# Two output projections in the other order, and the memory's rows in another buffer: a hybrid decoder block in float32 on one core

## The reference

```
hn = rms_norm(h)
z, xbc, dt, q, k, v, qi, ki, wi, g_ssd, g_attn = split(hn @ w_in)
y_ssd  = ssd_branch(z, xbc, dt)          # 256 x 2048, normed in 4 groups
y_attn = dsa_branch(q, k, v, qi, ki, wi) # 256 x 1024
merged = sigmoid(g_ssd) * (y_ssd @ w_ssd_o) + sigmoid(g_attn) * (y_attn @ w_attn_o)
h += merged @ w_out
mn = rms_norm(mem)                       # 256 memory tokens
h += cross_attention(rms_norm(h), mn, w_cq, w_ckv, w_co)
h += hier_moe(rms_norm(h))               # 4 groups of 8 experts, top 1 group, top 2 experts
```

## Time and profile before

| | us |
|---|---|
| median of 3 runs | 1519.66 |
| lowest, highest | 1517.8, 1520.55 |
| the profiled execution | 1519.16 |
| its span in the profile | 1517.3 |
| TensorE busy in the span | 1381.7 (91%) |
| VectorE, ScalarE busy | 845.1 (56%), 386.7 (25%) |
| mean granted clock of TensorE | 0.977 |

### The profile page before, as it was taken

How to read it: one execution, slowest core, us unless ns; L and a number is a source line. 1 busy time by engine, 2 the same in 40 slices (tenths; PEclk the granted TensorE clock), 3 DMA queues, 4 the chain that set the end, 5 groups by cost and what they waited for, 6 DMA issues and landing times. The chain is left out here.

```text
span 1517.3 us, 23993 instructions
## 1 busy us (share of the span) xinstructions
PE 1381.7 (91%) x9670; PEld 1096.5 (72%) x9670; DVE 845.1 (56%) x1613; ACT 386.7 (25%) x875; POOL 70.5 (5%) x65
## 2 busy tenths in 40 slices
PE   8999999999999998767699999999999989887674
PEld 7888888899998554334288888888999985534241
DVE  5587878677974342112165878886679643322022
ACT  2222567511111121001122235675020021111001
POOL 0000520000000000000000014100000000000000
PEclk9999999999999999899999999999999999999898
DMA  8434443336551789999963445333384509999995
GB/s 311 164 125 167 166 172 112 114 136 248 178 171 56 297 342 419 418 415 416 380 239 129 149 181 181 139 112 112 112 305 159 166 14 366 372 417 416 416 418 241
DMA packets 119262, 358.56 MB, mean 236 GB/s; under 512 B 12016, under 2 KB 14448, under 8 KB 103792
## 3 DMA queue, kind: packets, MB, share of 16 engines
q1 hardware_dynamic: 118608, 354.93, 61.1%
q0 software_dynamic: 544, 2.10, 0.3%
HBM read 355.89 MB, written 1.11 MB: 235 GB/s over the span
## 5 line engine op out<-in xcount | busy, mean ns | idle before, releaser
L867 PE MATMUL bank<-hT,wring 128*128 128x256 f32 x896 | 196.2, 380 | 0.0
L867 PEld LDWEIGHTS bank<-hT,wring 128*128 128x128 f32 x896 | 169.3, 190 | 23.9 <-issue 0.7
L1227 PE MATMUL bank<-wring,big 128*32 128x256 f32 x1536 | 100.8, 421 | 37.5 <-DMA wring<-in_w_up_e 22.4
L1227 PEld LDWEIGHTS bank<-wring,big 128*32 128x32 f32 x1536 | 51.2, 121 | 85.3 <-DMA wring<-in_w_up_e 25.1
L2185 DVE TENSOR_TENSOR h<-bank,h 128x512 f32<-128x512 f32 x64 | 44.2, 691 | 120.2 <-PE bank L1283 120.2
L2176 DVE TENSOR_TENSOR big<-bank,big 128x256 f32<-128x256 f32 x16 | 6.8, 425 | 149.3 <-ACT big L1522 149.3
L1778 DVE SCALAR_TENSOR_TENSOR scr<-bank,prm,scr 128x255 f32<-128x255 f32 (+1 forms) x144 | 62.7, 477 | 47.2 <-ACT scr L1349 44.5
L898 PE MATMUL bank<-hT,wring 128*128 128x128 f32 x736 | 86.9, 276 | 0.8 <-DVE btok L1639 0.8
L898 PEld LDWEIGHTS bank<-hT,wring 128*128 128x128 f32 x736 | 84.2, 192 | 3.4 <-issue 2.1
L898 PE MATMUL bank<-big,wring 128*128 128x128 f32 x704 | 81.3, 275 | 4.1 <-ACT big L1381 3.8
L1181 PE MATMUL bank<-big,xn 128*128 128x256 f32 x256 | 73.1, 444 | 12.0 <-DVE big L2087 12.0
(11 more groups left out here) (360 smaller groups left out, 2321.5 us busy)
## 6 DMA issues: line engine op xcount, KB each, us to landing
wring<-in_w_in SPq DMA_DIRECT2D x68, 1024.0 KB, 7.0
wring<-in_w_gate_e SPq DMA_DIRECT2D x14, 4096.0 KB, 19.9
wring<-in_w_up_e SPq DMA_DIRECT2D x14, 4096.0 KB, 23.6
wring<-in_w_ssd_o SPq DMA_DIRECT2D x16, 1024.0 KB, 6.1
wring<-in_w_ckv SPq DMA_DIRECT2D x16, 1024.0 KB, 7.3
scr<-in_w_down_e SPq DMA_DIRECT2D x8, 2048.0 KB, 26.7
ga<-in_w_down_e SPq DMA_DIRECT2D x8, 2048.0 KB, 31.2
qq<-in_w_down_e SPq DMA_DIRECT2D x8, 2048.0 KB, 26.6
```

The costliest lines, as they stand in the source:

```text
L867: ins = nc.tensor.matmul(bank[bank_of(job)][:, i * SEQ:(i + 1) * SEQ], wring[:, SLOT[c], k, m:m + P], src[:, k, :], start=n == 0, stop=n = ...
L1227: ins = nc.tensor.matmul(bank[b][j * S:(j + 1) * S, i * F:(i + 1) * F], x[:, k, e:e + S], up_part[i][:, j, k * F:(k + 1) * F], start=k == ...
```

## The change

The output projection of the attention comes ahead of the state space part's. The new order is: sums `att`, `atto` 0, sums `y`, `atto` 1, `ssdo` 0, `mem`, `ssdo` 1, sums `merged`. `atto` becomes the one whose `put` writes `mgT`, `ssdo` the one that adds. `FIRST_OF` now names `att`: its first three weight sums go to `xs`, where yT's transposes read, and wait for the last of these. `wo` waits for `ssdo`'s products in place of `atto`'s. The memory's rows go to `mix` in place of `big`; POOL waits for the last gate product's combination and the last `pv` in place of `ssdo` 1. The 2 MB of expert rows that go to `mix` are loaded after the chunk of `cq` 0 in place of `wo` 0, and wait for the last `memT`. The second weight sum of `atto` lies 2048 columns into its buffer in place of 1024.

```diff
--- before.py
+++ after.py
@@ -125,7 +125,7 @@
         if m >= 6:
             o += [("yT", i) for i in range(4 * m - 24, 4 * m - 20)]
     o += [("join", GATES[3], 1), ("sigmoid", 0)]
-    o += [("sums", "y"), ("ssdo", 0), ("ssdo", 1), ("sums", "att"), ("atto", 0), ("mem",), ("atto", 1), ("sums", "merged")]
+    o += [("sums", "att"), ("atto", 0), ("sums", "y"), ("atto", 1), ("ssdo", 0), ("mem",), ("ssdo", 1), ("sums", "merged")]
     o += [("memT", i) for i in range(4)] + [("sums", "mem"), ("wo", 0), ("wo", 1)]
     o += [("norm", 1), ("ck", 0)] + [("hT", 1, i) for i in range(4)] + [("ck", 1), ("sums", "h")]
     o += [("cv", 0), ("cv", 1), ("cq", 0), ("cq", 1)]
@@ -174,7 +174,7 @@
 EARLY = ("q", "z", "gate")
 UNITS = [st[1] if st[0] == "part" else st for st in ORDER
          if st[0] in SEVEN or st[0] == "part" and st[1][0] in SEVEN and st[2] == 0]
-FIRST_OF = {"h0": (("qi",), (1, 2)), "y": (("ssdo", 0), (1, 2, 3))}
+FIRST_OF = {"h0": (("qi",), (1, 2)), "att": (("atto", 0), (1, 2, 3))}
 INPUTS = [st[1] for st in ORDER if st[0] == "sums"]
 
 
@@ -351,7 +351,7 @@
         xbcT = cols(big, 0, CC, SEQ)
         zt = cols(big, 0, TT, DI)
         yT = cols(big, 0, 2 * KC, SEQ)
-        memx = cols(big, 0, TT, D)
+        memx = cols(mix, 0, TT, D)
         memT = cols(big, 2048, KC, SEQ)
         xg = cols(big, 0, KC, E * S)
         sel = cols(big, 2048, TT, E * S)
@@ -432,6 +432,8 @@
                 return cols(ga, 0, KC // 2, HALF_W), cols(ga, 1024, KC // 2, HALF_W)
             if st[0] == "ssdo":
                 return cols(spare_slot, 0, KC, HALF_W), cols(spare_slot, 2048, KC, HALF_W)
+            if st[0] == "atto":
+                return cols(spare_slot, 0, KC // 2, HALF_W), cols(spare_slot, 2048, KC // 2, HALF_W)
             return cols(spare_slot, 0, KC // 2, HALF_W), cols(spare_slot, 1024, KC // 2, HALF_W)
 
         up_part = [wring[:, 2 * i:2 * i + 2, :, :].rearrange("p (w j) k n -> p w j (k n)", w=1).rearrange("p w j (h m) -> p w (j h) m", h=2)[:, 0]
@@ -723,13 +725,12 @@
                     for n in ahead_of.get(c, ()):
                         acum_to_all(l, n)
                     chunk(l, c, before)
-                    if c == CHUNK[(("wo", 0), 0)]:
-
-                        filled(sp, l, JOB[(("atto", 0), 1)])
+                    if c == CHUNK[(("cq", 0), 0)]:
+
+                        filled(sp, l, JOB[(("memT", 3), 0)])
                         settle(sp)
                         src = w_down[l, 1, 0:BE].rearrange("j (k p) n -> p k j n", p=P)
                         sp.dma_start(mix_rows, src[:, 0]).then_inc(mix_in, 16)
-                    if c == CHUNK[(("cq", 0), 0)]:
 
                         drained(sp, l, JOB[(GATES[3], 4)])
                         settle(sp)
@@ -799,7 +800,8 @@
                 for t in range(TT):
                     power(l * NORMS + 2 + t, st_[:, 8 + t * SG:8 + (t + 1) * SG])
 
-                filled(pool, l, JOB[(("ssdo", 1), PRODUCTS[-1])])
+                drained(pool, l, JOB[(GATES[3], 4)])
+                filled(pool, l, JOB[(("pv", len(PAIRS) - 1), 0)])
                 settle(pool)
                 pool.dma_start(memx, mem.rearrange("(t p) d -> p t d", p=P)).then_inc(mem_in, 16)
                 pool.wait_ge(mem_sq, l + 1)
@@ -1071,7 +1073,7 @@
                 elif kind == "atto":
                     seven(l, st, {1: [JOB[(("pv", len(PAIRS) - 1), 0)]]} if st[1] == 0 else {}, by_channel=True)
                 elif kind == "wo":
-                    made = {1: [JOB[(("atto", 0), PRODUCTS[-1])]], 2: [JOB[(("atto", 1), 3)]], 4: [JOB[(("atto", 1), PRODUCTS[-1])]]}
+                    made = {1: [JOB[(("ssdo", 0), PRODUCTS[-1])]], 2: [JOB[(("ssdo", 1), 3)]], 4: [JOB[(("ssdo", 1), PRODUCTS[-1])]]}
                     seven(l, st, made if st[1] == 0 else {})
                 elif kind == "memT":
                     pe.wait_ge(mem_rdy, l + 1)
@@ -1426,7 +1428,7 @@
                 elif kind == "mem":
                     act.wait_ge(mem_in, l * 16 + 16)
                     for t in range(TT):
-                        ins = nc.scalar.activation(cols(big, 2048, TT, D)[:, t, :], memx[:, t, :], ACT.Square, scale=D ** -0.5,
+                        ins = nc.scalar.activation(cols(mix, 2048, TT, D)[:, t, :], memx[:, t, :], ACT.Square, scale=D ** -0.5,
                                                    accum_out=st_[:, 20 + t:21 + t])
                     ins.then_inc(mem_sq, 1)
                     act.wait_ge(mem_rstd, l + 1)
@@ -1934,7 +1936,7 @@
                         whole = wholes[(a + b) % 2]
                         link(V.tensor_tensor(whole, x, y, op))
                         of = whole.rearrange("p (c t) -> p c t", t=P)
-                        if g == 0:
+                        if g == 1:
                             return V.tensor_tensor(mgT[:, rows, ts], of, gateT[g][:, rows, ts], ALU.mult)
                         link(V.tensor_tensor(of, of, gateT[g][:, rows, ts], ALU.mult))
                         return V.tensor_tensor(mgT[:, rows, ts], mgT[:, rows, ts], of, ALU.add)
@@ -1969,7 +1971,7 @@
                     if made:
                         all_drained(dve, l, [JOB[(m, 0)] for m in made])
                     if st[1] == "merged":
-                        drained(dve, l, JOB[(("atto", 1), PRODUCTS[-1])])
+                        drained(dve, l, JOB[(("ssdo", 1), PRODUCTS[-1])])
                     x11, x12, x21, x22 = quarters(source_of[st[1]])
                     to = sums_of[st[1]]
                     at = (l * len(INPUTS) + INPUTS.index(st[1])) * 4
@@ -1980,6 +1982,8 @@
                     V.tensor_tensor(one_of(to, 3), x12, one_of(to, 1), ALU.subtract).then_inc(xsum_rdy, 1)
                     V.tensor_tensor(one_of(to, 2), x11, x21, ALU.subtract).then_inc(xsum_rdy, 1)
                     if st[1] in FIRST_OF:
+                        if st[1] == "att":
+                            filled(dve, l, JOB[(("yT", 7), 0)])
                         weight_sums(l, *FIRST_OF[st[1]])
                 elif kind in ("ck", "cq"):
                     to = {"ck": ckT, "cq": qT}[kind]
```

## The result

| | before | after |
|---|---|---|
| median of the runs made side by side (5 each) | 1519.06 | 1510.90 |
| lowest, highest | 1517.8, 1520.55 | 1510.31, 1511.76 |
| profiled execution, its span | 1519.16, 1517.3 | 1511.41, 1509.6 |

The changed kernel is faster: ratio 0.9946, 95% interval 0.9933 to 0.9958, 8.2 us by the medians. Two more comparisons of the same two kernels gave 0.9951 and 0.9957, so by the ratios the gain is 8.2, 7.4 and 6.5 us. The forecast was 1515.5, give or take 1.6 in its likeliest case, in a range up to 1519.3.

What follows compares the result with a forecast made beforehand. TensorE, its matmuls filling 91% of the span, was taken to bound the mixer half, DMA the expert stages. Twice 2.07 us, 4.14, with all else at nothing, took the median from 1519.66 to 1515.5 +- 1.6; the range reached 1519.3.

Steps and rivals of the forecast that it cites:

- The hole, 2.07 us per layer: After yT's last transposes: without TensorE's 1.90 us idle, the first product starts at 302.42 in place of 304.49.
- Product 5's cover of 0.9 us: `atto` 0, product 5: VectorE's first sum of weights is ready at 305.1, 0.9 us before TensorE wants it.
- Product 4's of 1.2 us: `atto` 1, product 4: VectorE's fourth sum of weights is ready at 324.4, 1.2 us before it is wanted at 325.6.
- rivals 1 and 3: 1: part of gain lost waiting for VectorE, 1517.5, chance 0.18; 3: VectorE's queue holds `atto` 1's fourth weight sum, 1523, 0.07.
- Rival 4: Start of `atto`: it still waits for yT, through a bank; held excluded, chance nothing.
- POOL's issue beside VectorE's sums: At about 301: POOL's 0.96 us issue of the memory's rows beside VectorE's sums of qT, charged at nothing.
- SP's queue, the 2 MB for `mix`: Weight chunks follow the new order; the 2 MB for `mix` moves from `wo` 0 to `cq` 0: cost none.
- Expert stage shifts with TensorE: Expert stages' loads, issued on TensorE's events from 502.48, start 2.07 us earlier and end so much earlier.
- rival 2: Expert stage, DMA share 0.99, swallows the 4.14 us as idle ahead of it; time near 1519.5, chance 0.08.
- TensorE is saved nothing, because memT isn't late now: Earlier issue of the memory's rows, about 301 in place of 355.39: no gain for TensorE.
- all that it costs today: Layer 1, product 4 of `ck` 0: the 0.25 us wait for VectorE's sum (L1610) is such waits' whole present cost.
- The hole costs its length and nothing in clock: Window 300 to 305: granted clock 1.00 around TensorE's 1.90 us of idle, so no extra cost in clock.

Runs made afterwards that it cites:

- wait_layer0: Changed kernel with `atto` 0 again waiting for yT's last copy, in layer 0 alone: median 1514.97 us, ratio 0.9979 to the kernel before.
- wait_layer1: Changed kernel with `atto` 0 again waiting for yT's last copy, in layer 1 alone: median 1513.78 us, ratio 0.9969 to the kernel before.
- after_wait_yT: Changed kernel with `atto` 0 again waiting for yT's last copy in both layers: median 1518.25 us, ratio 0.9999 to the kernel before.
- mem_step_later: Kernel before with the work on the memory's rows moved behind `atto` 1: median 1517.20 us, ratio 0.9991 to the unedited kernel before.
- memory_alone: Kernel before in its old projection order, with only the memory's part of the change: median 1517.14 us, ratio 0.9990 to the unedited kernel before.
- before_again: Kernel before, unchanged, run and profiled once more: median 1518.18 us, ratio 0.9995.
- before_third: Kernel before, unchanged, a third profile: one execution, 1518.57 us.
- filler_2us_layer1: Changed kernel with 17 transposes of the identity ahead of `atto` 0 in layer 1: median 1514.25 us, ratio 0.9968 to the kernel before.

## Why the prediction was right in part

- **The hole, 2.07 us per layer:** right. 1.80 us from transposes to product, both layers, to the hundredth. The block behind it is 0.07 us shorter per layer as well. wait_layer0, wait_layer1 and after_wait_yT show it by undoing it alone.
- **Product 5's cover of 0.9 us:** right, 0.96. **Product 4's of 1.2 us:** right, 1.6. So rivals 1 and 3 (a wait for VectorE's sums, of part of the gain or of more than all) did not come: no wait for L1612 stands in TensorE's list. Rival 4 (a wait through a bank) neither.
- **POOL's issue beside VectorE's sums, charged at nothing:** right. It runs from 300.35 for 0.96 us, and the sums that start at 300.17 and 300.90 take 0.69 each, as before. The lock of which the Trainium skill, "SBUF — State Buffer", section "SBUF: two separate sides", tells shows no effect here: by this trace neither sum was held by the issue.
- **SP's queue, the 2 MB for `mix`:** right at nothing. The expert rows land in 13.6 us, `wo`'s in 9.6, nobody waits for them.
- **Expert stage shifts with TensorE** (rival 2: it swallows the gain): right. The downs' issue moved to 499.30; the 500.4 forecast less the 0.97 of this execution's start is 499.4.
- **"TensorE is saved nothing, because memT isn't late now":** wrong, and the first of the two failed steps. I asked whether `memT` waited, and not who else stood behind the memory in ScalarE's queue. VectorE did, 2.7 us in layer 0 and 3.5 in layer 1, and the second costs TensorE 1.18 us. mem_step_later and memory_alone show the cause in their traces: each takes the wait out and TensorE's steps are 3.45 again. Their times can't tell a gain of that size. I had read the 0.25 us of L1610 as "all that it costs today"; the rest stands in no list of waits.
- **"The hole costs its length and nothing in clock":** wrong, the second. It was true of the one execution I had (the clock of 300 to 305 was 1.00). In before_again, before_third and memory_alone the clock falls just behind the hole, for 1.63 us. In the sum it is the term of the hole that was too small: both holes together cost 6.7 us by the medians, not 4.14. How much of that surplus is this fall and how much are falls further on is shown by the profiles alone, as follows.

How much of 6.5 to 8.2 us this makes: 4.14 for the holes' length; 0.8 for the wait in `wo` (1.18 us in two of three profiles of the kernel before); 0.7 for the fall behind the hole (1.63 us in three of seven). That is 5.6 us, each term seen in rows. The first two are undone by edits; the third is absent from all executions without the hole. The profiled pair's 7.75 has a fall at 542 (1.47) and the start (0.97) in it instead, both of that pair of executions alone.

The profiles hold the rest as well. I compared the mean of the three of the kernel before with the mean of the four of the kernel after, stretch by stretch: 7.21 us of span in all. 4.27 are the holes with the 0.07 us behind each; 1.09 the fall behind layer 0's (two of three); 0.80 `wo` in layer 1 (two of three); 0.78 the stretch from the downs' issue to layer 1 (falls at 542 and 761, one each, about 1.4 us each); 0.32 the start. All other stretches together make under 0.1.

**What stays open.** Whether those last two, 1.1 us, belong to the change. The start does not by what was seen: its values overlap (22.74 to 23.82 against 22.76 to 23.37). For the falls, place in time speaks for it: the wait of 2.48 us ahead of layer 1 lies earlier from the clock's rise in all four profiles of the changed kernel than in any with a fall but one (filler_2us_layer1, 741.9). The order is not a simple one, since the same wait at 745.5 and 746.6 (before, before_third) brought none. And no run moved that wait alone, and three or four profiles don't give a rate. Filling the holes gave back 0.5 and 0.8 us by the medians, which their intervals don't tell from nothing. And after_wait_yT, which has both holes but the memory's part too, should have kept some 0.8 us and kept 0.2, with 1.4 either way.

No version tried is measurably faster than the changed kernel.

## What to carry to other kernels

A move that takes TensorE's own idle time out gave its length here and more, and the sum of the measured durations foretold the new starts to some tenths of a microsecond. Price an early load by everything that stands behind its first reader in that engine's queue, and compare the steps from start to start: delays of 0.1 to 0.3 us stand in no list of waits and made 1.2 us here. Where a median is to be foretold to 0.2%, one profile is too few, since each has its own start and its own falls of the clock, of 1.4 to 1.6 us each here; take two or three of the same kernel before calling a hole free of a cost in clock, and note in each when the clock rose: here that told the executions that fell from those that didn't.

## What the runs showed of the hardware

- The granted clock can fall to its lower level for 3.4 us behind an idle time of TensorE of 1.90 us, and needn't: 3 of 7 executions did, with the same rows ahead of it. The three had the clock up from 10.36 to 11.73 us at the start, the four others from 12.84 to 13.25. At a later place it fell behind 1.84 us in one execution and not behind 1.69 in another.
- The clock's rise at the start of the program came at 10.36, 11.73 and 13.25 us in three executions of one and the same kernel, and moved everything behind it by up to 1.1 us.
- With 17 transposes into a free bank (2.02 us) in that place, the clock stayed up in the two executions profiled, in which it rose at 12.68 and 13.34 us; whether they kept it up is not shown. The median with them was within what could be measured of that with the idle time (0.9995).
